# Retention layer of a hybrid encoder: the decay mask built by another engine, and three changes of order

## The reference, cut to what matters

```python
proj = x @ w_in                          # q, k (4 x 256), v, g (4 x 512)
q, k = rope(q), rope(k)
# scores[n, m] = q_n . k_m * 256**-0.5 * mask(n - m)
# mask(d) = exp(lg_fwd * d)  for d >= 0,  exp(lg_bwd * -d)  for d < 0
o = scores @ v                           # forward and backward scan, summed
y = (o - mean(o)) / sqrt(var(o) + 1e-5) * ret_norm_g     # for each head
out = (silu(g) * y) @ w_out
```

## Time and profile before

| | |
|---|---|
| median of 3 runs | 1358.67 us (1358.38 to 1358.68) |
| the profiled execution | 1357.12 us, of which its instructions span 1355.3 us |
| granted TensorE clock | 0.998 |
| busy share of the span | PE 98%, PEld 87%, DVE 72%, ACT 42%, POOL 14% |
| the retention, from the span's start | about 577 to 945 us; head 0 to 664, heads 1 to 3 of some 77 us each |
| chain that ended last | PE 82%, DVE 11%, ACT 2%, DMA 2%, POOL 1% |

### The profile page before, as it was taken

The page is one execution under the profiler, slowest core; times in us unless marked ns, Lnnn a source line. Parts: engine busy times, 40 slices in busy tenths (PEclk is TensorE's granted clock), DMA queues, the critical chain, the costliest instruction groups (busy, mean ns, idle before and its releaser), DMA issues.

```text
span 1355.3 us, 19504 instructions
## 1 busy us (share of the span) xinstructions
PE 1332.8 (98%) x7880; PEld 1180.4 (87%) x7880; DVE 978.8 (72%) x1211; ACT 564.0 (42%) x723; POOL 195.0 (14%) x161
## 2 busy tenths in 40 slices
PE   9999999999999999999999999989999999999997
PEld 8887878999999988898878878878899999998885
DVE  5999957998888533567877788763289988875336
ACT  3468834534434222334334444433144344343221
POOL 4011114111111000160313104000041111100001
PEclk9999999999999999999999999999999999999999
DMA  6210113233333432152123140242322333333221
GB/s 226 65 60 1 32 63 100 88 110 108 94 118 98 142 107 93 62 202 75 50 94 125 63 155 31 94 180 70 110 76 94 111 107 93 120 121 102 105 80 62
DMA packets 86352, 131.74 MB, mean 97 GB/s; under 512 B 2832, under 2 KB 61456, under 8 KB 86160
## 3 DMA queue, kind: packets, MB, share of 16 engines
q1 hardware_dynamic: 86288, 130.84, 29.2%
HBM read 126.63 MB, written 4.19 MB: 97 GB/s over the span
## 4 chain that ended last, share of the span: by engine, by line
PE 82%; DVE 11%; ACT 2%; DMA 2%; POOL 1%; issue 1%; DVEq 0%; SPq 0%; ACTq 0%; POOLq 0%
PE ps L1873 20%; PE ps L1875 20%; PE ps L1874 20%; PE ps L1951 19%; DVE w_lo L1718 2%; DMA raw<-in_l_w_in 2%; DVE acc L1262 2%; DVE w_lo L424 1%; POOL w_lo L424 1%; ACT w_hi L420 1%; PE ps L2128 1%; PE ps L1886 1%; DVE raw L1767 0%; DVE raw L1792 0%; DVE x_tok L1502 0%
## 5 line engine op out<-in xcount | busy, mean ns | idle before, releaser
L1873 PE MATMUL ps<-xT_hi,w_hi 128*128 128x256 f32 (+1 forms) x992 | 302.3, 305 | 0.5 <-POOL w_lo L424 0.5
L1875 PE MATMUL ps<-xT_hi,w_lo 128*128 128x256 f32 (+1 forms) x992 | 301.1, 304 | 0.0
L1874 PE MATMUL ps<-xT_lo,w_hi 128*128 128x256 f32 (+1 forms) x992 | 301.1, 304 | 0.0
L424 DVE TENSOR_TENSOR w_lo<-raw,w_hi 128x2048 fp32r<-128x2048 f32 x44 | 101.1, 2298 | 186.6 <-ACT w_hi L420 186.4
L1873 PEld LDWEIGHTS ps<-xT_hi,w_hi 128*128 128x128 f32 x992 | 189.5, 191 | 8.8 <-POOL w_lo L424 1.1
L1875 PEld LDWEIGHTS ps<-xT_hi,w_lo 128*128 128x128 f32 x992 | 189.5, 191 | 7.5
L1874 PEld LDWEIGHTS ps<-xT_lo,w_hi 128*128 128x128 f32 x992 | 189.6, 191 | 7.4
L420 ACT ACTIVATE w_hi<-raw 128x2048 fp32r<-128x2048 f32 x50 | 95.7, 1914 | 212.6 <-PE ps L1951 151.7
L988 ACT ACTIVATE sum_hi<-w_sum 128x1536 fp32r<-128x1536 f32 x38 | 56.5, 1488 | 183.4 <-PE ps L1875 182.7
L1873 PE MATMUL ps<-mix_hi,sum_hi 128*128 128x256 f32 x456 | 129.0, 283 | 0.0
L1874 PE MATMUL ps<-mix_lo,sum_hi 128*128 128x256 f32 x456 | 129.0, 283 | 0.0
(11 more groups left out here) (250 smaller groups left out, 2770.8 us busy)
## 6 DMA issues: line engine op xcount, KB each, us to landing
raw<-in_l_w_in SPq DMA_DIRECT2D x33, 1024.0 KB, 5.2
raw<-in_l_ffn_w_gate SPq DMA_DIRECT2D x22, 1024.0 KB, 5.3
raw<-in_l_ffn_w_up SPq DMA_DIRECT2D x22, 1024.0 KB, 5.3
raw<-in_l_ffn_w_down SPq DMA_DIRECT2D x22, 1024.0 KB, 4.9
raw<-in_l_w_out SPq DMA_DIRECT2D x12, 1024.0 KB, 5.1
x_tok<-in_x SPq DMA_DIRECT2D x4, 512.0 KB, 6.9
x_kept<-x_tok SPq DMA_DIRECT2D x1, 2048.0 KB, 9.1
x_tok<-x_kept SPq DMA_DIRECT2D x4, 512.0 KB, 7.4
```

The lines of the kernel that those rows point to most:

```text
L424: eng.tensor_tensor(w_lo[ch.s][:], raw[ch.s][:], f32(w_hi[ch.s][:]), ALU.subtract)\
L1873: nc.tensor.matmul(dst, a[0], b[0], start=start, stop=False, skip_group_check=goes_on)
L1874: nc.tensor.matmul(dst, a[0], b[1], start=False, stop=False, skip_group_check=goes_on)
L1875: return nc.tensor.matmul(dst, a[1], b[0], start=False, stop=stop, skip_group_check=goes_on)
```

## The change

1. The mask: GpSimd only writes the distances. ScalarE makes both sides from them with Relu (of the distances negated and as they are) and takes the exponential of each with its decay as the scale (`decays`). VectorE multiplies the two (`decays_joined`). On ScalarE the four instructions stand where `mask_exp(0)` was in head 0, and after the second split of k in the others.
2. SyncE: the load of the first value block stands ahead of the wait for x and of the rotary tables, the spill behind the second value block.
3. Order on ScalarE in heads 1 to 3: the second split of p2 ahead of the copy `u2_copied`, which also waits for the mask now, and each split of p3 ahead of a rotary split of k.
4. The last head: ScalarE and VectorE split tiles 0 and 1 of y after all four mask tiles, and VectorE norms the last head ahead of its split of `C_OUT1 + 1`.

```diff
@@ sync
             for c in range(2):
                 load(sp, Chunk(C_RET + c), W1[:, :, D * c:D * c + 256])
-            sp.wait_ge(x_normed, 8 * 2)
-            sp.dma_start(rope1[:], ins["rope1"]).then_inc(rope1_landed, 16)
-            sp.dma_start(x_kept, x_tok[:]).then_inc(x_spilled, 16)
...
             for c in range(4):
                 load(sp, Chunk(C_RET + 2 + c), value_or_gate(0, c // 2, c % 2))
                 if c == 0:
+                    sp.wait_ge(x_normed, 8 * 2)
+                    sp.dma_start(rope1[:], ins["rope1"]).then_inc(rope1_landed, 16)
+                if c == 1:
+                    sp.dma_start(x_kept, x_tok[:]).then_inc(x_spilled, 16)
                     load_step(1, "a11", value_or_gate(1, 0, 0))
@@ gpsimd
-            def exponents(h):
+            def distances(h):
                 if h:
                     pool.wait_ge(ret_masked, 4 * h)
-                if h == 1:
-                    pool.wait_ge(xmix_lo_made, 4)
-                mine(nc.gpsimd.iota(mask[:], ...))
-                mine(nc.gpsimd.tensor_scalar(mask_b[h][:], mask[:], 0.0, None, ALU.min))
-                mine(nc.gpsimd.tensor_tensor(mask_b[h][:], mask_b[h][:], decay[:, 1, h:h + 1].broadcast_to([P, SPAN]), ALU.mult))
-                mine(nc.gpsimd.tensor_scalar(mask[:], mask[:], 0.0, None, ALU.max))
-                mine(nc.gpsimd.tensor_tensor(mask[:], mask[:], decay[:, 0, h:h + 1].broadcast_to([P, SPAN]), ALU.mult))
-                nc.gpsimd.tensor_tensor(mask[:], mask[:], mask_b[h][:], ALU.subtract).then_inc(exponent_made, 1)
+                nc.gpsimd.iota(mask[:], ...).then_inc(distance_made, 1)
@@ scalar
-            def mask_exp(h):
-                act.wait_ge(exponent_made, h + 1)
-                nc.scalar.activation(mask[:], mask[:], ACT.Exp).then_inc(mask_made, 1)
+            def decays(h):
+                act.wait_ge(distance_made, h + 1)
+                if h == 1:
+                    act.wait_ge(xmix_lo_made, 4)
+                nc.scalar.activation(mask_b[h][:], mask[:], ACT.Relu, scale=-1.0).then_inc(side_made, 1)
+                act.wait_ge(side_made, 2 * h + 1)
+                nc.scalar.activation(mask[:], mask[:], ACT.Relu).then_inc(side_made, 1)
+                nc.scalar.activation(mask_b[h][:], mask_b[h][:], ACT.Exp, scale=decay[:, 1, h:h + 1])
+                act.wait_ge(side_made, 2 * h + 2)
+                nc.scalar.activation(mask[:], mask[:], ACT.Exp, scale=decay[:, 0, h:h + 1]).then_inc(decays_made, 1)
@@ scalar, first_head
                 for half in range(2):
                     rotated_hi(0, 1, half)
-                mask_exp(0)
+                decays(0)
                 make_hi(act, Chunk(C_RET + 4))
@@ scalar, head
-                mask_exp(h)
                 step_hi(h, "p6", 0)
...
                 step_hi(h, "k", 1)
+                decays(h)
                 step_hi(h, "p2", 0)
+                step_hi(h, "p2", 1)
                 act.wait_ge(ret_used, done(h, "p6"))
+                act.wait_ge(mask_made, h + 1)
                 nc.scalar.activation(y_pair(h, 0), ps[:, X_BANKS, :], ACT.Copy).then_inc(u2_copied, 1)
-                step_hi(h, "p2", 1)
                 step_hi(h, "p7", 0)
                 step_hi(h, "p7", 1)
+                step_hi(h, "p3", 0)
                 rotated_hi(h, 1, 0)
+                step_hi(h, "p3", 1)
                 rotated_hi(h, 1, 1)
-                step_hi(h, "p3", 0)
-                step_hi(h, "p3", 1)
...
                 for kt in range(TT):
                     scores_hi(h, kt)
-                    if h == RH - 1 and kt == 1:
-                        y_tile_hi(0)
-                        y_tile_hi(1)
@@ scalar, after the heads
+            y_tile_hi(0)
+            y_tile_hi(1)
             make_hi(act, Chunk(C_OUT1))
@@ vector
+            def decays_joined(h):
+                dve.wait_ge(decays_made, h + 1)
+                nc.vector.tensor_tensor(mask[:], mask[:], mask_b[h][:], ALU.mult).then_inc(mask_made, 1)
@@ vector, first_head
                 nc.vector.tensor_tensor(m_b12, m_b22, m_b12, ALU.subtract).then_inc(xmix_made, 1)
+                decays_joined(0)
@@ vector, head
                 rotated_lo(h, 0)
+                decays_joined(h)
                 step_lo(h, "p2", 0)
...
-                if h == RH - 1:
-                    y_tile_lo(0)
-                    y_tile_lo(1)
                 masked(h, 2)
@@ vector, after the heads
+            y_tile_lo(0)
+            y_tile_lo(1)
             make_lo(dve, Chunk(C_OUT1))
             y_tile_lo(2)
             y_tile_lo(3)
+            gated(RH - 1)
             make_lo(dve, Chunk(C_OUT1 + 1))
-            gated(RH - 1)
```

More of the change, by code:

```diff
@@ L330, in build_encoder @@
         rv_lo_made = sem("rv_lo_made")
-        exponent_made = sem("exponent_made")
         mask_made = sem("mask_made")
@@ L362, in build_encoder @@
         gate34_made = sem("gate34_made")
+        distance_made = sem("distance_made")
+        side_made = sem("side_made")
+        decays_made = sem("decays_made")
         y_turned = sem("y_turned")
@@ L716, in _ @@
             pool.wait_ge(x_normed, 8 * 2)
-            def exponents(h):
+            def distances(h):
                 if h:
                     pool.wait_ge(ret_masked, 4 * h)
-                if h == 1:
-                    pool.wait_ge(xmix_lo_made, 4)
-                mine(nc.gpsimd.iota(mask[:], pattern=[[1, SPAN]], base=-(SEQ - P), channel_multiplier=-1,
-                                    allow_small_or_imprecise_dtypes=True))
-                mine(nc.gpsimd.tensor_scalar(mask_b[h][:], mask[:], 0.0, None, ALU.min))
-                mine(nc.gpsimd.tensor_tensor(mask_b[h][:], mask_b[h][:], decay[:, 1, h:h + 1].broadcast_to([P, SPAN]), ALU.mult))
-                mine(nc.gpsimd.tensor_scalar(mask[:], mask[:], 0.0, None, ALU.max))
-                mine(nc.gpsimd.tensor_tensor(mask[:], mask[:], decay[:, 0, h:h + 1].broadcast_to([P, SPAN]), ALU.mult))
-                nc.gpsimd.tensor_tensor(mask[:], mask[:], mask_b[h][:], ALU.subtract).then_inc(exponent_made, 1)
+                nc.gpsimd.iota(mask[:], pattern=[[1, SPAN]], base=-(SEQ - P), channel_multiplier=-1,
+                               allow_small_or_imprecise_dtypes=True).then_inc(distance_made, 1)
             def inverse_deviations(h):
@@ L737, in inverse_deviations @@
                         .then_inc(o_rstd, 1)
-            exponents(0)
+            distances(0)
             inverse_deviations(0)
-            exponents(1)
-            exponents(2)
+            distances(1)
+            distances(2)
             inverse_deviations(1)
-            exponents(3)
+            distances(3)
             inverse_deviations(2)
```

## The result

The changed kernel takes **1349.42 us** (median of 4 runs, 1349.30 to 1349.75) against 1358.53 for the kernel before on the same chip (1358.31 to 1358.68): a ratio of 0.9933, 95% interval 0.9916 to 0.9951. The forecast was 1351.1 us, with a range from 1348.3 to 1354.6. The profiled execution took 1349.30 us (span 1347.5); the sum of the prediction, made against the profiled execution before, was 1349.6.

What follows compares the result with a forecast made beforehand. TensorE was taken as busy nearly throughout, so only its pauses could yield time. Gains of 0.55 + 1.8 + 2.4 + 2.8 = 7.55 us off 1357.12 gave 1349.6, plus 1.55 for the median: 1351.1 us, range 1348.3 to 1354.6.

Steps and rivals of the forecast that it cites:

- Pause a: TensorE's 1.37 us pause in head 0 until the first value block is split; the earlier load was to remove it.
- head 0 pays: Rival: ScalarE's longer queue ahead of head 0's gate block costs 2 us more than forecast, 1353.1 us; chance 0.12.
- the load gains nothing: Rival: something else holds the first value block back, so head 0 loses 2 us, 1353.7 us; chance 0.05.
- one wait for another: Rival: p3's splits delay rotary splits, or the mask's wait delays p7's; 4.2 us of gains vanish, 1355.3 us; chance 0.06.
- b: TensorE's 1.73 us pause in head 1 until p6 is split; to go without GpSimd's five instructions, 1.8 us gained.
- hole ahead of p2: ScalarE's 6.73 us idle wait for p2's weights in head 2; to cover the mask's 5.2 us, leaving 1.5.
- slower: Rival: mask work beyond 9.0 us stops TensorE at p2 in each of three heads, 1361.4 us; chance 0.03.
- The order of p3: Heads 1 to 3: p3's split moved ahead on ScalarE lets VectorE split p3 1.7 us earlier, gaining 2.4 us.
- c: TensorE's pauses ahead of p3 and p4 in heads 1 to 3, 0.2 to 0.5 us each, 1.9 together; to go.
- d: TensorE's 1.19 us pause between the last head's mask tiles; to go once y tiles 0 and 1 come later.
- e: TensorE's pauses of 2.10 and 1.1 us for the last head's norm; 1.6 us were to remain.
- everything closes: Rival: the pauses left in head 0 (0.8 us) and at the norm (1.6) go too, 1348.7 us; chance 0.1.

Runs made afterwards that it cites:

- padded kernels: The changed kernel with the mask's first Relu done four or eight more times in heads 1 to 3: 1349.60 us with four, 1359.38 with eight.
- last version: The changed kernel with head 0's mask made before the value splits and other TensorE products placed in the last norm's wait: 1346.53 us.

## Why the prediction was right, and where it was not

**The spill: right.** The load was forecast for the time when its buffer comes free; it is issued at 577.33. The first value split was put at 597.35; it starts at 597.21, 0.16 of which is the execution's own lead. Pause a is gone, and the kernel with the spill in its old place has it.

**The mask in head 0: right.** Four instructions and the load take 614.83 to 619.95, 5.12 us (5.15 forecast); the product of the sides 1.09 (1.09, by the column); the first mask product comes at 628.62 (628.9), the first scores by values at 630.84 (631.0). Of 1.37 us 0.50 stayed (0.55). The Trainium skill ("ScalarE: Activation LUTs", section "What ACT_TABLE_LOAD costs") puts a drain of 1380 ns on top of the table load, by which head 0 would have lost. The trace shows none of it: the load starts 0.02 us after the Relu, ends at 618.05, and the exponential starts at 618.07. The rivals *head 0 pays* and *the load gains nothing* fall with these rows, and *one wait for another* with the list of waits, which has none for p3, p2 or p7.

**The mask in heads 1 to 3: right, its cover too small.** b gave 1.79 (1.8), by the way described, and comes back with GpSimd's five instructions. The hole ahead of p2 took in ScalarE's four, with 1.26 us over. The rival *slower* set its limit at 9.0 us of mask work, at p2; the padded kernels show no loss at 9.1 and put the limit near 11.1 at p2 and near 10.0 at p7, which the prediction took to be safe by some 10 us. At p2 the split began 6.48 us later than in the changed kernel (701.02 and 694.54) and TensorE lost 1.93, so it comes some 4.5 us after the split could be ready and not 2.3.

**The order of p3: the step failed.** "With it in front, VectorE splits p3 straight after the second rotation, 1.7 us earlier": that alone was to close c. Undone beside the new mask it costs nothing; the order closes c by itself only where the old mask stays (2.8 us). The new mask removes the cause earlier in the head: GpSimd slowed the sum and the splits at the head's start, s2 came later, and with it the weights of k and p2. The prediction looked for that contention in head 1 alone and took head 2's s2 of 2.29 us in the earlier trace rows as a sign that GpSimd was quiet there; but GpSimd had been at that head's mask until 11 us before. So GpSimd's arithmetic stands behind b and, together with the old order, behind c. The sum came out even so, since the pauses were counted once, whichever edit closes them: 2.76 (2.4).

**The last head: right in its traces.** d closes; the norm begins at 894.94, which with the 5.21 us won until then is 900.15 on the clock of the trace before (900.0 forecast). d and e gave 2.63 (2.8); 1.93 of e are left (1.6).

**From the profile to the median: wrong.** "The median of the runs is 1.55 above it" was carried over as if it belonged to every kernel. The runs tie it to pause e. The sum hit the profiled execution (1349.6 forecast, 1349.30 measured), and the medians fell by 9.1 us instead of 7.6, because the runs after lie where their profile lies. Nine kernels without the long pause, four runs each, spread by 0.2 to 0.9 us, with medians within 0.6 us of their profiles; the kernel with the last head's old order, which has it, spreads by 2.5 (five runs). At e TensorE stands idle for most of 3 us, and its granted clock can then fall to 0.50 for some 3 us. The Trainium skill ("TensorE: Matmul & The Clock Gate", Part 1) names 1.2 GHz as the level after idling, with 426.7 ns between matmuls of 512 columns; the rows agree (0.43 us). Of the three profiled executions with the long pause the clock fell there in two; in none of those without it did it fall there. That this makes the whole offset is not shown: filling the pause took 1.24 us off the median, but the interval includes no change.

The rival *everything closes* (1348.7) is not what happened, but the last version shows that it could be had: both pauses left were order, not work.

One slip is in the chances: the forecast, the first three rivals and nearly all of the fourth add up to some 0.94, not to the 0.92 given for faster.

## What to carry to other kernels

Price a pause of TensorE by the clock behind it too: look at the granted clock just after the pause in more than one execution, and don't carry an offset between profile and runs over to a kernel that no longer has the pause. Where one engine slows another, follow the slowed results through the loads that wait for them: the same contention can stand in the trace as two different waits, tens of microseconds apart. And when two edits could each close a wait, undo them singly and together before giving either the credit.

## What the runs showed of the hardware

Behind a short sequence of pauses of TensorE (2.1 us, four transposes, 1.1 us) the granted clock fell from 1.00 to 0.50 in one profiled execution of a program and not in another; where it fell, it cost 1.4 to 1.5 us. VectorE's two-tensor instructions beside GpSimd's arithmetic took up to 1.8 times as long (four splits 8.32 us against 4.7, a sum 4.02 against 2.29). Beside GpSimd's distances a sum was not slowed: in the kernel before it took 2.28 us from 666.79, and the distances 0.89 from 667.01. Relu of 896 columns took 0.93 to 0.96 us on ScalarE, an exponential with a scale per partition 1.03 to 1.05, and the second Relu, which waits for the first, started 0.04 us after the end of the first.
